# Differences of decay sums on POOL and more convolution taps on VectorE, in a two-layer GLA, convolution and MoE trunk

## The chip, the cores and the metric

The kernel runs on one core of one Trainium2 chip. The metric is the device time of one execution in microseconds (us), given as the median of several runs. The engines are named as in the profile: PE is TensorE (matmul), PEld its weight loads, DVE is VectorE, ACT is ScalarE, POOL is GpSimd, SP is SyncE.

## What is computed

Two layers over 256 tokens of width 1024, all in float32. Each layer runs a token mixer and then a channel mixer (a dense SwiGLU in layer 0, a top-2-of-8 mixture of experts in layer 1). The change lies in the token mixer, which is, cut to what matters:

```
z = h @ w_in                        # q, k, v, g, gate rank, ca, cb
log_a = log_sigmoid(gr @ w_gate_up + b_gate) / 16
bc = cumsum(log_a)                  # "decay sums", along the tokens
decay[i, j] = exp(bc_i - bc_j)      # for j <= i
attn = einsum(q, k, decay);  o = attn @ v (+ carried state);  o = rmsnorm(o) * silu(g)

u = ca * sigmoid(cb)                # 512 channels
u = causal_dwconv(u, conv_w) + b    # 31 taps, each channel by itself
u = silu(layernorm(u))
x = x + concat([o, u]) @ w_out
```

## The kernel before

**Weights.** Every weight is loaded by SP in units of 1 MB. ACT copies a unit to `w_hi` (L463), DVE writes the remainder to `w_lo` (L755, `lo(n)`, a `tensor_tensor` whose two inputs both lie in SBUF), and PE multiplies with both. The mixer has ten input units (`in_unit`, `tokens`) and four output units (`down_unit`).

**Attention by levels.** The masked attention of a layer is put together from nine levels, `LEVELS = [128, 64, 32, 16, 8, 4, 2, 1, 0]`. For level n the decay sums `cum` (128 x 512) are cut in blocks of 2s, and every element is subtracted from, or has subtracted from it, the block's reference element. `differences(n)` does this with two instructions of 128 x 256 (L832, L833; one instruction, L825, for n = 0), so 15 instructions in a layer. ACT takes the exponential in place (`decays(n)`, L503), DVE multiplies q by it (`q_decayed(n)`, L841, 128 x 512), POOL multiplies k by it (L423, 128 x 512), PE forms the products (`level(n)`, L1336). The first three results go out through ACT, the levels 3 to 8 through DVE (`level_read_out(n)`, L852: two `copy_predicated`, data from PSUM, mask from SBUF). After level 8 is read out, PE multiplies the attention by v (L1380 to L1382).

**Convolution.** The 512 channels are four tiles. A tap on DVE is one `scalar_tensor_tensor` of 128 x 256 (L810: `acc = cu * tap + acc`, `cu` and `acc` in SBUF; the first tap of a tile is L806). A tap on PE is a matmul of a diagonal matrix, which ACT makes (L544), with the input (L1312, two records a tap). DVE has all 31 taps of the tiles 0 and 1 and the first 19 of tile 2; PE has 12 of tile 2 and all 31 of tile 3, so 43. Every DVE tap waits for the tap before it on the same tile (`conv_step[c]`).

**What sets the order.** Each engine's program is written out by hand. In DVE's program of a mixer, `lo`, `q_decayed`, `differences`, `conv_input` (L796), `level_read_out` and batches of taps `conv(count)` alternate; PE's program has `conv(3)` behind levels 2 to 7, `conv(4)` behind level 8, `conv(16)` behind the products with v, and the remainder behind the transposes (L1390). POOL's program of a mixer is the eight multiplications of k, and two loads of norm weights. `Difs` and `qkE` have two buffers each, used by even and odd n, so that `differences(n)` waits until q and k of level n - 2 are multiplied.

**Around the end of the mixer.** When the products with v are done: ACT squares them (L605), DVE sums (L922), ACT takes the root (L609), DVE scales and gates (L932), PE transposes (L1390), ACT and DVE write `t_hi` and `t_lo` (L612, L937), and PE starts the output projection (`down_unit`, L1259). In the middle of the first output unit PE sums the convolution's channels (L1401) and for that all taps must be done.

Of the kernel before, what the change touches and what calls it, by code (L numbers as in the profile page):

```python
# [21 lines left out]
ALU = mybir.AluOpType  # L22
# [3 lines left out]
P = 128  # L26
# [8 lines left out]
def trunk(nc, x, ln1_w, w_in, w_gate_up, b_gate, gla_norm_w, conv_w, conv_b, cn_w, cn_b, w_out,  # L35
          ln2_w, wd_gate, wd_up, wd_down, w_router, we_gate, we_up, we_down, final_norm_w, out):
    _, T, D = x.shape
# [3 lines left out]
    TAPS, CH = conv_w.shape[1:]  # L41
# [51 lines left out]
    with ctx:  # L93
# [3 lines left out]
        def on(stack):  # L97
# [171 lines left out]

        BY_VECTOR = 19
        LATE = TAPS - BY_VECTOR
        DVE_CONV = ([(c, w) for w in range(LATE) for c in (0, 1)]
                    + [(c, w if c < 2 else w - LATE) for w in range(LATE, TAPS) for c in (0, 1, 2)])
        PE_CONV = [(3, w) for w in range(TAPS)] + [(2, w) for w in range(BY_VECTOR, TAPS)]
        STEPS = [TAPS, TAPS, BY_VECTOR + 1, 1]
        IN_BANK = [0, 1, 2, 0, 1, 2, 0, 1, 2, 0]
# [100 lines left out]
        def _(pool):  # L379
# [32 lines left out]
            for l in range(L):  # L412

                if l:
                    pool.wait_ge(added, 2 * TT)
                pool.memset(cu[:, :, 0:PAD], 0.0).then_inc(pads_ready, 1)
                pool.memset(att[:], 0.0).then_inc(pads_ready, 1)

                for n in range(len(LEVELS) - 1):
                    pool.wait_ge(decay_ready, 8 * l + n + 1)  # L420
                    if n >= 2:
                        pool.wait_ge(level_done, 9 * l + n - 1)
                    pool.tensor_tensor(qkE[n % 2][:, 1], qk[:, 1], Difs[:, n % 2], ALU.mult).then_inc(kE_ready, 1)  # L423
                pool.wait_ge(level_done, 9 * (l + 1))
                pool.dma_start(lnw[:], norm_weights[2 * l + 1].partition_broadcast(P)).then_inc(lnw_ready, 16)
                pool.wait_ge(normed, TT * (2 * l + 2))
                pool.dma_start(lnw[:], norm_weights[2 * l + 2].partition_broadcast(P)).then_inc(lnw_ready, 16)
# [319 lines left out]
        def _(dve):  # L747
            def lo(n, item=None):

                slot, _ = slot_use(n)  # L750
                if item is None:
                    dve.wait_ge(hi_ready, n + 1)
                else:
                    dve.wait_ge(hi_ready, item * N_FF + (n + 1))
                dve.tensor_tensor(w_lo[slot][:], raw[slot][:], w_hi[:, hi_slot(n), :].bitcast(F32), ALU.subtract).then_inc(lo_ready, 1)  # L755
# [34 lines left out]
            def mixer(l):  # L790
                b = BASE[l]

                def conv_input(g):
                    dve.wait_ge(cgate_ready, 2 * l + g + 1)
                    dve.wait_ge(pads_ready, 2 * (l + 1))
                    dve.tensor_tensor(cu[:, 2 * g:2 * g + 2, PAD:], cgate, WB[IN_BANK[U_C + 2 * g]][:].rearrange("p (c t) -> p c t", c=2),  # L796
                                      ALU.mult).then_inc(cu_ready, 1)
# [3 lines left out]
                def conv(count):  # L801

                    for c, w in DVE_CONV[done[0]:done[0] + count]:
                        if w == 0:
                            dve.wait_ge(cu_ready, 2 * l + c // 2 + 1)
                            dve.tensor_scalar(acc[:, c, :], cu[:, c, 0:T], taps[:, l, 0, c:c + 1],  # L806
                                              pv[:, l, PV_CB + c:PV_CB + c + 1], ALU.mult, ALU.add).then_inc(conv_step[c], 1)
                        else:
                            dve.wait_ge(conv_step[c], STEPS[c] * l + w)
                            dve.scalar_tensor_tensor(out=acc[:, c, :], in0=cu[:, c, w:w + T], scalar=taps[:, l, w, c:c + 1],  # L810
                                                     in1=acc[:, c, :], op0=ALU.mult, op1=ALU.add).then_inc(conv_step[c], 1)
                    done[0] += count


                def differences(n):

                    s = LEVELS[n]
                    Dif = Difs[:, n % 2]
                    if n == 0:
                        dve.wait_ge(cum_ready, l + 1)  # L820
                    if n >= 2:
                        dve.wait_ge(kE_ready, 8 * l + n - 1)
                        dve.wait_ge(qE_ready, 8 * l + n - 1)
                    if s == P:
                        dve.tensor_tensor(Dif[:, :, 0:P], cum[:, :, P - 1:P].broadcast_to([P, KT, P]), cum[:, :, 0:P],  # L825
                                          ALU.subtract).then_inc(dif_ready, 1)
                        return
                    nb = KT * T // (2 * s)
                    blocks = cum[:].rearrange("p k (b s) -> p (k b) s", s=2 * s)
                    dst = Dif.rearrange("p k (b s) -> p (k b) s", s=2 * s)  # L830
                    ref = blocks[:, :, s - 1:s].broadcast_to([P, nb, s])
                    dve.tensor_tensor(dst[:, :, 0:s], ref, blocks[:, :, 0:s], ALU.subtract)  # L832
                    dve.tensor_tensor(dst[:, :, s:], blocks[:, :, s:], ref, ALU.subtract).then_inc(dif_ready, 1)  # L833

                def q_decayed(n):
                    dve.wait_ge(decay_ready, 8 * l + n + 1)
                    if n == 0:
# [37 lines left out]
                        c = cum[:, k, P * t:P * (t + 1)]  # L875
                        ins = dve.tensor_tensor_scan(c, ones[:], c, 0.0, ALU.mult, ALU.add)
                ins.then_inc(cum_ready, 1)
                differences(0)
                differences(1)
                lo(b + 7)  # L880
                q_decayed(0)
                lo(b + 8)
                q_decayed(1)
                conv_input(0)
                conv(6)
                differences(2)
                lo(b + 9)
                conv(4)
                q_decayed(2)
                differences(3)  # L890
                lo(b + 10)
                conv(4)
                conv_input(1)
                q_decayed(3)
                differences(4)
                conv(6)
                lo(b + 11)
                q_decayed(4)
                differences(5)
                conv(8)  # L900
                lo(b + 12)
                level_read_out(3)
                q_decayed(5)
                differences(6)
                conv(7)
                lo(b + 13)
                level_read_out(4)
                q_decayed(6)
                differences(7)
                conv(10)  # L910
                level_read_out(5)
                q_decayed(7)
# [287 lines left out]
        def _(pe):  # L1200
# [79 lines left out]
            def mixer(l):  # L1280
# [25 lines left out]
                def conv(count):  # L1306

                    for c, w in PE_CONV[done[0]:done[0] + count]:
                        m = len(PE_CONV) * l + done[0]
                        bank = WB[3][:, 0:T] if c == 3 else WB[3][:, T:2 * T]  # L1310
                        pe.wait_ge(diag_ready, m + 1)
                        pe.matmul(bank, diag[:, done[0] % DIAGS, :], cu[:, c, w:w + T], start=(w in (0, BY_VECTOR) and (c == 3) == (w == 0)),  # L1312
                                  stop=(w == TAPS - 1)).then_inc(diag_used, 1)
                        done[0] += 1
# [66 lines left out]
                    pe.matmul(WB[1][:, vs], attx[:, r, hp, :], v[:, 0, vs], start=True, stop=False)  # L1381
                    ins = pe.matmul(WB[1][:, vs], att[:, r, 2 + hp, :], v[:, 1, vs], start=False, stop=True)  # L1382
                ins.then_inc(o_done, 1)
                conv(16)
                pe.wait_ge(o_gated, l + 1)
                for hd in range(HEADS):
                    for t in range(TT):
# [182 lines left out]
```

## Time and profile before

| | |
|---|---|
| median of 3 runs | 1306.63 us (1305.07 to 1307.05) |
| the profiled execution, its own time | 1306.7 us |
| its span from first to last instruction | 1304.9 us |
| busy share of the span | PE 96%, PEld 82%, DVE 79%, ACT 64%, POOL 6% |
| mean granted clock of TensorE | 0.983 of full |
| mixer of layer 0, by the timeline | roughly 16 to 145 us |
| mixer of layer 1, by the timeline | roughly 354 to 480 us |

The engine's busy share is over the whole span: the mixers take about a fifth of it, the dense channel mixer and the experts the rest. In a timeline row the first number is the start and the second the duration, both in us; an engine's neighbouring instructions of one kind are merged into a row (x6), and then the second number reaches from the first one's start to the last one's end. DVE instructions of this kernel overlap their neighbours by some 0.08 us.

### The profile page before, as it was taken

The page shows a single profiled execution, that of the slowest core. Times are in us where ns is not written, and L with a number is a line of the kernel's source. Part 1 is how long each engine was busy: PE and PEld are TensorE (multiplying, and loading weights), DVE is VectorE, ACT ScalarE, POOL GpSimd, SP SyncE. Part 2 cuts the span into 40 slices and gives each one's busy share as a digit, 9 for nine tenths or more (in the row PEclk, how much of TensorE's full clock was granted, in tenths as well). Part 3 has the DMA queues.
Part 4 walks back from the last instruction along what each step waited for, and adds up shares of the span by engine and source line. Part 5 has one row for each costly group of instructions (what it writes and reads, how often), then busy time and mean ns, then how long its engine had stood idle before and what let it go on. Part 6 is the DMA issues. An engine that isn't in the chain of part 4 may idle for free.

```text
span 1304.9 us, 18713 instructions
## 1 busy us (share of the span) xinstructions
PE 1251.0 (96%) x6911; PEld 1067.8 (82%) x6911; DVE 1036.2 (79%) x963; ACT 832.4 (64%) x755; POOL 84.4 (6%) x75
## 2 busy tenths in 40 slices
PE   5998899999799987999999999999999999999997
PEld 5997799999699876888888888888888888888885
DVE  5898654444569967989989989989989989989986
ACT  5754643333476545677677677677677677677674
POOL 3250000000013100000000000000000000000000
PEclk9999899999899998999999999999999999999998
DMA  9940455555434234999999999999999999999970
GB/s 275 331 130 17 145 187 174 189 194 176 147 102 158 82 129 146 337 386 355 335 388 353 336 387 354 338 385 354 337 386 353 338 385 354 340 384 352 338 292 32
DMA packets 180166, 351.69 MB, mean 270 GB/s; under 512 B 8678, under 2 KB 68380, under 8 KB 180124
## 3 DMA queue, kind: packets, MB, share of 16 engines
q1 hardware_dynamic: 178108, 343.77, 75.3%
q0 software_dynamic: 2016, 7.34, 1.5%
q8 instruction: 29, 0.48, 0.2%
q14 instruction: 13, 0.11, 0.0%
HBM read 348.99 MB, written 2.10 MB: 269 GB/s over the span
## 4 chain that ended last, share of the span: by engine, by line
PE 90%; DVE 7%; ACT 2%; issue 1%; DMA 0%; SPq 0%; DVEq 0%; ACTq 0%
PE YB L1517 19%; PE WBS L1504 12%; PE WBS L1505 12%; PE WBS L1506 12%; PE YB L1259 8%; PE WBS L1222 5%; PE WBS L1223 5%; PE WBS L1224 5%; DVE w_lo L755 2%; PE WBS L1312 2%; DVE acc L810 2%; PE YB L1532 1%; PE WBS L1271 1%; PE YB L1336 1%; PE WBS L1234 1%
## 5 line engine op out<-in xcount | busy, mean ns | idle before, releaser
L755 DVE TENSOR_TENSOR w_lo<-raw,w_hi 128x2048 fp32r<-128x2048 f32 x325 | 741.1, 2296 | 113.1 <-ACT w_hi L463 109.6
L463 ACT ACTIVATE w_hi<-raw 128x2048 fp32r<-128x2048 f32 x325 | 616.4, 1915 | 143.8 <-PE WBS L1506 67.2
L1504 PE MATMUL WBS<-w_hi,t_hi 128*128 128x512 f32 (+1 forms) x768 | 290.6, 378 | 2.0 <-DVE t_lo L1152 2.0
L1505 PE MATMUL WBS<-w_lo,t_hi 128*128 128x512 f32 (+1 forms) x768 | 285.8, 372 | 0.0
L1506 PE MATMUL WBS<-w_hi,t_lo 128*128 128x512 f32 (+1 forms) x768 | 285.7, 372 | 0.0
L1504 PEld LDWEIGHTS WBS<-w_hi,t_hi 128*128 128x128 f32 x768 | 144.5, 188 | 26.8 <-issue 2.1
L1506 PEld LDWEIGHTS WBS<-w_hi,t_lo 128*128 128x128 f32 x768 | 144.4, 188 | 26.3
L1505 PEld LDWEIGHTS WBS<-w_lo,t_hi 128*128 128x128 f32 x768 | 144.6, 188 | 24.4
L1222 PE MATMUL WBS<-t_hi,w_lo 128*128 128x256 f32 x544 | 157.3, 289 | 6.5 <-DVE w_lo L755 4.9
L1223 PE MATMUL WBS<-t_hi,w_hi 128*128 128x256 f32 x544 | 156.2, 287 | 0.0
L1224 PE MATMUL WBS<-t_lo,w_hi 128*128 128x256 f32 x544 | 156.0, 287 | 0.0
L1517 PE MATMUL YB<-w_hi,eT_hi 128*128 128x512 f32 x352 | 114.6, 407 | 1.0
L1222 PEld LDWEIGHTS WBS<-t_hi,w_lo 128*128 128x128 f32 x544 | 106.8, 196 | 9.1 <-issue 7.9
L1517 PE MATMUL YB<-w_lo,eT_hi 128*128 128x512 f32 x352 | 111.0, 396 | 0.0
L1517 PE MATMUL YB<-w_hi,eT_lo 128*128 128x512 f32 x352 | 110.8, 396 | 0.0
L1223 PEld LDWEIGHTS WBS<-t_hi,w_hi 128*128 128x128 f32 x544 | 106.9, 197 | 0.4
L1224 PEld LDWEIGHTS WBS<-t_lo,w_hi 128*128 128x128 f32 x544 | 106.8, 196 | 0.0
L1517 PEld LDWEIGHTS YB<-w_hi,eT_hi 128*128 128x128 f32 x352 | 62.0, 188 | 25.0 <-issue 13.9
L1517 PEld LDWEIGHTS YB<-w_hi,eT_lo 128*128 128x128 f32 x352 | 66.4, 189 | 16.2
L1517 PEld LDWEIGHTS YB<-w_lo,eT_hi 128*128 128x128 f32 x352 | 66.2, 188 | 16.2
L665 ACT ACTIVATE dT_hi<-dact 128x512 fp32r<-128x512 f32 x11 | 7.0, 632 | 111.2 <-PE YB L1259 106.3
L810 DVE SCALAR_TENSOR_TENSOR acc<-cu,taps,acc 128x256 f32<-128x256 f32 x156 | 71.4, 524 | 0.0
(243 smaller groups left out, 1324.1 us busy)
## 6 DMA issues: line engine op xcount, KB each, us to landing
raw<-in_we_gate SPq DMA_DIRECT2D x88, 1024.0 KB, 5.3
raw<-in_we_up SPq DMA_DIRECT2D x88, 1024.0 KB, 5.3
raw<-in_we_down SPq DMA_DIRECT2D x88, 1024.0 KB, 5.2
raw<-in_w_in SPq DMA_DIRECT2D x20, 1024.0 KB, 5.5
raw<-in_wd_gate SPq DMA_DIRECT2D x11, 1024.0 KB, 5.4
raw<-in_wd_up SPq DMA_DIRECT2D x11, 1024.0 KB, 5.3
raw<-in_wd_down SPq DMA_DIRECT2D x11, 1024.0 KB, 4.8
raw<-in_w_out SPq DMA_DIRECT2D x8, 1024.0 KB, 11.0
```

What stands on the lines that cost most here:

```text
L463: act.activation(w_hi[:, hi_slot(n), :], raw[slot][:], ACT.Copy).then_inc(hi_ready, 1)
L755: dve.tensor_tensor(w_lo[slot][:], raw[slot][:], w_hi[:, hi_slot(n), :].bitcast(F32), ALU.subtract).then_inc(lo_ready, 1)
L810: dve.scalar_tensor_tensor(out=acc[:, c, :], in0=cu[:, c, w:w + T], scalar=taps[:, l, w, c:c + 1], in1=acc[:, c, :], op0=ALU.mult, op1=ALU ...
L1222: pe.matmul(dst, lo[:, k, cols], a_hi[:, k, :], start=(k == 0), stop=False)
L1223: pe.matmul(dst, hi[:, k, cols], a_hi[:, k, :], start=False, stop=False)
L1224: ins = pe.matmul(dst, hi[:, k, cols], a_lo[:, k, :], start=False, stop=(k == KD - 1))
L1259: ins = pe.matmul(YB[:, 2 * t + half, :], a[:, k0 + k, tok], w[:, k, HALF * half:HALF * (half + 1)], start=(first and k == 0 and s), stop= ...
L1312: pe.matmul(bank, diag[:, done[0] % DIAGS, :], cu[:, c, w:w + T], start=(w in (0, BY_VECTOR) and (c == 3) == (w == 0)), stop=(w == TAPS - ...
L1504: pe.matmul(bank, xs_hi[:, k0 + k, :], hi[:, k, :], start=start, stop=False)
L1505: pe.matmul(bank, xs_hi[:, k0 + k, :], lo[:, k, :], start=False, stop=False)
L1506: ins = pe.matmul(bank, xs_lo[:, k0 + k, :], hi[:, k, :], start=False, stop=stop)
L1517: ins = pe.matmul(YB[:, half, :], a[:, f, :], w[:, k, HALF * half:HALF * (half + 1)], start=(first and s), stop=(last and e))
```

## The change

POOL issues the differences for all levels: 0 and 1 at the start of its mixer program, and `differences(n + 2)` right behind its multiplication of k at level n. They are the same instructions on the same data, with the same waits. DVE loses them. Tile 2 of the convolution has 27 taps on DVE in place of 19, so DVE has 89 taps in a layer (81 before) and PE 35 (43 before). The batches of taps in DVE's program grow: 67 taps stand ahead of the read-out of level 8, where there were 55, and 22 behind it, where there were 26. The last 8 taps are all on tile 2. PE's batch behind the products with v is 12 (16 before), and the last batch has 1 (5 before). ACT makes 35 diagonals (43 before).

```
-        BY_VECTOR = 19
-        LATE = TAPS - BY_VECTOR
-        DVE_CONV = ([(c, w) for w in range(LATE) for c in (0, 1)]
-                    + [(c, w if c < 2 else w - LATE) for w in range(LATE, TAPS) for c in (0, 1, 2)])
+        BY_VECTOR = 27
+        LATE = 12
+        DVE_CONV = [(c, w) for w in range(LATE) for c in (0, 1)]
+        for w in range(BY_VECTOR):
+            DVE_CONV += [(c, w + LATE) for c in (0, 1) if w + LATE < TAPS] + [(2, w)]
...
 (POOL's program)
+                def differences(n):
+                    s = LEVELS[n]
+                    Dif = Difs[:, n % 2]
+                    if n >= 2:
+                        pool.wait_ge(kE_ready, 8 * l + n - 1)
+                        pool.wait_ge(qE_ready, 8 * l + n - 1)
+                    if s == P:
+                        pool.tensor_tensor(Dif[:, :, 0:P], cum[:, :, P - 1:P].broadcast_to([P, KT, P]), cum[:, :, 0:P],
+                                           ALU.subtract).then_inc(dif_ready, 1)
+                        return
+                    nb = KT * T // (2 * s)
+                    blocks = cum[:].rearrange("p k (b s) -> p (k b) s", s=2 * s)
+                    dst = Dif.rearrange("p k (b s) -> p (k b) s", s=2 * s)
+                    ref = blocks[:, :, s - 1:s].broadcast_to([P, nb, s])
+                    pool.tensor_tensor(dst[:, :, 0:s], ref, blocks[:, :, 0:s], ALU.subtract)
+                    pool.tensor_tensor(dst[:, :, s:], blocks[:, :, s:], ref, ALU.subtract).then_inc(dif_ready, 1)
+
+                pool.wait_ge(cum_ready, l + 1)
+                differences(0)
+                differences(1)
                 for n in range(len(LEVELS) - 1):
                     pool.wait_ge(decay_ready, 8 * l + n + 1)
                     if n >= 2:
                         pool.wait_ge(level_done, 9 * l + n - 1)
                     pool.tensor_tensor(qkE[n % 2][:, 1], qk[:, 1], Difs[:, n % 2], ALU.mult).then_inc(kE_ready, 1)
+                    if n + 2 < len(LEVELS) - 1:
+                        differences(n + 2)
...
 (DVE's program: its own differences() is gone, and of the order)
-                differences(0)
-                differences(1)
                 lo(b + 7)
                 q_decayed(0)
                 lo(b + 8)
                 q_decayed(1)
                 conv_input(0)
+                conv(8)
+                lo(b + 9)
                 conv(6)
-                differences(2)
-                lo(b + 9)
-                conv(4)
                 q_decayed(2)
-                differences(3)
                 lo(b + 10)
-                conv(4)
+                conv(6)
                 conv_input(1)
                 q_decayed(3)
-                differences(4)
-                conv(6)
+                conv(8)
                 lo(b + 11)
                 q_decayed(4)
-                differences(5)
-                conv(8)
+                conv(10)
                 lo(b + 12)
                 level_read_out(3)
                 q_decayed(5)
-                differences(6)
-                conv(7)
+                conv(9)
                 lo(b + 13)
                 level_read_out(4)
                 q_decayed(6)
-                differences(7)
                 conv(10)
...
 (PE's program, behind the products with v)
-                conv(16)
+                conv(12)
```

## Rows read from the trace of the kernel before

**Rows 1.** The page: the chain that ended last, by engine.
```profile
PE 90%; DVE 7%; ACT 2%; issue 1%; DMA 0%; SPq 0%; DVEq 0%; ACTq 0%
```

**Rows 2.** Windows: length, busy us of PE, PEld, DVE, ACT, POOL, clock, DMA.
```profile
75.00:90.00 15.00, 15.00 (x129) 14.17 (x128) 15.00 (x25) 5.50 (x11) 7.01 (x3) 1.00 0.43 141
...
105.00:110.00 5.00, 3.08 (x18) 2.78 (x17) 5.00 (x12) 0.74 (x2) 0.00 (x0) 0.80 0.31 108
```

**Rows 3.** Timeline of DVE, and one row of ACT, layer 0.
```profile
46.04 2.29 DVE L755 TENSOR_TENSOR w_lo<-raw,w_hi 128x2048 fp32r<-128x2048 f32 x1 [0.58 <-ACT w_hi L463]
...
49.96 3.38 DVE L755 TENSOR_TENSOR w_lo<-raw,w_hi 128x2048 fp32r<-128x2048 f32 x1
...
55.23 1.67 DVE L810 SCALAR_TENSOR_TENSOR acc<-cu,taps,acc 128x256 f32<-128x256 f32 x4
...
59.69 2.71 DVE L810 SCALAR_TENSOR_TENSOR acc<-cu,taps,acc 128x256 f32<-128x256 f32 x4
...
93.14 0.42 DVE L833 TENSOR_TENSOR Difs<-cum 128x256 f32<-128x256 f32 x1
93.48 4.04 DVE L810 SCALAR_TENSOR_TENSOR acc<-cu,taps,acc 128x256 f32<-128x256 f32 x10
93.60 0.63 ACT L503 ACTIVATE Difs<-Difs 128x512 f32<-128x512 f32 x1 [5.78 <-DVE Difs L833]
97.43 1.35 DVE L852 COPY_PREDICATED att<-masks,YB 128x512 f32<-128x512 uint8 x2
```

**Rows 4.** Timeline of POOL: multiplications of k, layers 0 and 1.
```profile
49.45 1.74 POOL L423 TENSOR_TENSOR lnw<-qk,Difs 128x512 f32<-128x512 f32 x1
58.31 2.61 POOL L423 TENSOR_TENSOR qkE<-qk,Difs 128x512 f32<-128x512 f32 x1 [7.12 <-ACT Difs L503]
...
71.26 6.09 POOL L423 TENSOR_TENSOR qkE<-qk,Difs 128x512 f32<-128x512 f32 x1 [4.24 <-ACT Difs L503]
...
94.37 4.29 POOL L423 TENSOR_TENSOR lnw<-qk,Difs 128x512 f32<-128x512 f32 x1 [2.18 <-ACT Difs L503]
...
434.84 1.28 POOL L423 TENSOR_TENSOR lnw<-qk,Difs 128x512 f32<-128x512 f32 x1 [6.42 <-PE YB L1336]
```

**Rows 5.** Timeline of POOL, mask building: s = 64, then s = 1.
```profile
3.24 0.25 POOL L400 TENSOR_SCALAR_AFFINE_SELECT mask_f<-mask_f 128x64 f32<-128x64 f32 x1
...
9.50 0.16 POOL L399 MEMSET mask_f<- 128x64 f32 x1
...
11.52 0.65 POOL L402 TENSOR_SCALAR_AFFINE_SELECT mask_f<-mask_f 128x64 f32<-128x64 f32 x1
```

**Rows 6.** Timeline of DVE and PE, layer 1, last levels.
```profile
434.73 1.36 DVE L852 COPY_PREDICATED att<-masks,YB 128x512 f32<-128x512 uint8 x2 [0.99 <-PE YB L1336]
...
444.58 0.46 PE L1380 MATMUL WBS<-v,att 128*128 128x128 f32 x2 [0.21 <-DVE att L852]
```

**Rows 7.** Timeline of PE: products with v, layer 0 and layer 1.
```profile
108.80 0.63 PE L1382 MATMUL WBS<-v,att 128*128 128x128 f32 x2
109.23 0.63 PE L1380 MATMUL WBS<-v,att 128*128 128x128 f32 x2
...
445.99 0.39 PE L1380 MATMUL WBS<-v,att 128*128 128x128 f32 x2
446.21 0.39 PE L1381 MATMUL WBS<-v,attx 128*128 128x128 f32 x2
```

**Rows 8.** Timeline of DVE and PE behind the products, layer 0.
```profile
118.07 2.46 DVE L810 SCALAR_TENSOR_TENSOR acc<-cu,taps,acc 128x256 f32<-128x256 f32 x6
119.14 1.04 PE L1390 MATMUL WBS<-ident,qk 128*128 128x128 f32 x8
...
121.36 1.28 DVE L937 SCALAR_TENSOR_TENSOR t_lo<-WBS,pv,t_hi 128x1024 fp32r<-128x1024 f32 x1 [0.83 <-ACT t_hi L612]
...
122.56 2.46 DVE L810 SCALAR_TENSOR_TENSOR acc<-cu,taps,acc 128x256 f32<-128x256 f32 x6
...
125.12 0.42 DVE L944 TENSOR_TENSOR acc<-acc,WBS 128x256 f32<-128x256 f32 x1
```

More of the change, by code:

```diff
@@ L812, in conv @@
                     done[0] += count
[L815 to L833, printed above, removed]
                 def q_decayed(n):
```

## The prediction

> **What bounds the kernel now.** I read the page first, for the chain that ended last: PE holds 90% of it and DVE 7% [rows 1]. PE's part is the experts and the dense mixer, which the change doesn't touch. So the question is where DVE's 7%, some 90 us, lies. The chain in order of time puts it in the two mixers: in layer 0 it runs on DVE from 48 us to 107 us without a break. The windows say the same: from 75 to 90 us DVE is busy 15.00 of 15.00 us, and from 105 to 110 us DVE is busy throughout, while PE is down to 3.08 of 5.00 us [rows 2]. In layer 0 the read-out of level 8 is therefore as late as DVE's work ahead of it is long, and PE's products with v wait for it. In layer 1 the two engines run neck and neck: DVE has one pause of 0.99 us, waiting for PE, and PE waits only 0.21 us for the last read-out [rows 6].
>
> Behind the mixers no one catches up what they lose: PE is the chain there. So what the mixers gain or lose is the kernel's.
>
> The third view was POOL's timeline, since POOL gets the work. A multiplication of 128x512 takes 1.28 us when DVE leaves it alone, but 1.74, 2.61, 4.29 and 6.09 us elsewhere [rows 4]. DVE shows the counterpart: four taps take 1.67 us, but 2.71 us where POOL's instruction of 58.31 us ends (at 60.92 us), and `lo` takes 2.29 us, but 3.38 us while POOL's second multiplication runs [rows 3, 4]. That is 1.04 and 1.09 us of standstill, nearly all of POOL's 1.28 us. So one POOL multiplication costs DVE about what it takes, and the two engines take turns. Only the read-outs (data from PSUM, one input in SBUF) run beside it at their usual pace: POOL's instruction of 94.37 us ends 1.23 us after the read-out of 97.43 us began, and that pair takes its usual 1.35 us [rows 3, 4].
>
> The Trainium skill states such a rule (SBUF — State Buffer, Who interferes with whom): a DVE instruction with two SBUF inputs and a GpSimd instruction that reads SBUF exclude each other for a whole instruction, the later one blocking. The trace agrees in the standstill of 1.04 and 1.09 us. It differs in the other direction: by that rule POOL would get its turn when the current DVE instruction ends, and its 6.09 us span several.
>
> **The change part by part, for one layer, up to the read-out of level 8.**
>
> Differences off DVE. One starts at 93.14 us and what follows it at 93.48 us, so one costs 0.34 us [rows 3]. The 12 of levels 2 to 7 stand in the gapless part: 12 x 0.34 = 4.1 us less. The first three stood ahead of a wait: `lo` at 46.04 us had waited 0.58 us for ACT's `w_hi` [rows 3], which starts no sooner, so they give nothing.
>
> Taps on DVE. Ten taps take 4.04 us with one lone tap at some 0.47, so each further one 0.396 us [rows 3]. Twelve more stand ahead of the read-out (67 for 55): 4.75 us more. DVE's own work ahead of the read-out is thus longer by 0.7 us. This alone shows that the differences were traded for taps one for one, and anything POOL takes comes on top.
>
> Differences on POOL. The trace has no POOL instruction of this form. From the nearest row, the multiplication with 512 elements and a standstill of 1.04 to 1.09 us, one of 256 elements blocks DVE for 0.52 us if all of it goes by the element, and for 1.07 us if nothing does. Alone a multiplication takes 1.28 us and blocks for most of it, so most goes by the element; I take 0.55 us. Twelve of them: 6.6 us. Some find cover in read-outs and in the two `conv_input` (PSUM data). A read-out pair is 1.35 us [rows 3], but the k multiplications already use some of these; I take off two diffs' and a bit's worth, 1.3 us: 5.3 us. The bounds are 12 x 0.52 with half of it covered, 3.1 us, and 12 x 1.07, 12.8 us. Of the first three, the last may still run when `lo` wants to start: 0.3 us (between 0 and 0.55).
>
> Short rows. At s = 1 the differences walk 256 rows of one element. POOL's memset at s = 1 takes 0.16 us, no sign of a cost; its affine select goes from 0.25 us at s = 64 to 0.65 us at s = 1, so 0.40 us for 63 more rows, 6.3 ns each [rows 5]. Over the levels 2 to 7 there are 2 x (8 + 16 + 32 + 64 + 128 + 256) = 1008 rows, so between 0 and 6.4 us. The select works out an index for each element, which a subtraction doesn't; I take a value near the memset's end, 0.5 us.
>
> Behind the products with v. PE's transposes start at 119.14 us, once its batch of 16 taps is through, though DVE's gating is over when the taps at 118.07 us start [rows 8]. With 12 taps they start up to 1.1 us sooner. But DVE's six taps there are now all on tile 2, each waiting for the last. The one such handover in view, from the last tap (122.56 + 2.46 = 125.02) to the addition at 125.12 [rows 8], has a gap of 0.10 us where neighbours otherwise overlap by 0.08. So each link costs about 0.12 to 0.18 us, five links 0.6 to 0.9 us. DVE's `t_lo`, which had waited 0.83 us for ACT [rows 8], is now late by DVE's own taps. What is left of the 1.1 us is 0.3 us. The remaining taps (2 for 6), PE's four fewer and ACT's eight fewer diagonals lie beside the output projection and give nothing: PE's first half unit covers them, and the channel sums follow it.
>
> Layer 0: 0.7 + 5.3 + 0.3 + 0.5 - 0.3 = +6.5 us.
>
> Layer 1 has the same terms, with two differences. DVE's pause of 0.99 us takes up 1.0 us of them. Against that, PE is no longer kept busy. In layer 0, where PE waited for DVE, the products with v ran at the lower granted clock (0.80 of full as the mean of 105 to 110 us [rows 2]), 0.43 us from group to group, and 0.22 us in layer 1 [rows 7]. If layer 1 comes to wait like layer 0, its groups run at the slower pace too: nearly nine of the twelve at 0.21 us more, 1.8 us. Layer 1: 6.5 - 1.0 + 1.8 = +7.3 us.
>
> The sum is made on the profiled execution's 1306.7 us (span 1304.9), within 0.1 us of the median: 1306.7 + 6.5 + 7.3 = 1320.5 us.
>
> The Trainium skill has a figure for POOL's rate (GPSIMD Engine Reference, section 3.1: 4497 ns for 2048 elements). With the row of 1.28 us for 512 that makes 2.1 ns an element, so 0.75 us for one difference as an estimate, of which some 0.6 us would block; the sum would be 1321 or 1322 us by it.
>
> **The rivals.**
>
> *POOL's chain becomes late (1334 us).* Each level now needs three turns of POOL in a row (k, and two differences two levels on), and POOL's waits for a turn reached 6.09 us [rows 4]. DVE needs some 7 to 8 us a level. If a turn is refused through a whole batch of taps, `q_decayed` stands still until the second difference (0.55), ACT's exponential (0.63) and a part of the k multiplication (1.28) are done [rows 3, 4]. That is some 2 us a level, of which 0.55 is counted already, so 1.3 to 1.4 us more on five levels, 6.7 us a layer: 1320.5 + 13.4 = 1334 us. For it: the batches of taps, where POOL was refused, grow from 6 to 8 and from 8 to 10. Against: while DVE stands still POOL gets its turn at once, so that it heals itself. Short rows at the select's price would end at about the same time (2 x 5.9 more, 1332 us). Together 0.27.
>
> *All of it is covered (1306 us).* If the differences fall in read-outs, `conv_input` and waits, +5.3 and the layer-1 clock go, and 2 x (0.7 + 0.5 - 0.3) - 1.0 is left, with 0.3 us twice: 1308 us; with links of taps at no cost 1306 us. It decides once 9 or more of 12 find cover. Against: the read-outs start only at level 3, and k multiplications fill them. 0.06.
>
> *Faster (1302 us).* The other side: POOL's new order pushes the k multiplications of levels 2 to 5, which stand DVE still now, into read-outs. Each is worth 1.04 us, three a layer would give 6 us against 1308. It needs all differences covered as well. 0.04.
>
> **How the numbers follow.** Forecast 0.63, late POOL or short rows 0.27, covered 0.06, faster 0.04. The forecast's own range: with 3.1 us in place of 5.3, no short rows and no loss of clock 1306.7 + 3.8 + 2.8 = 1313; with 0.75 us a difference and 2 us of short rows about 1328. The range that leaves out 2 in 10 goes from 1311 to 1337 us. Within 0.2% is 2.6 us, about what a measurement can tell. Faster 0.04, same 0.06, slower 0.90.
>
> **What would show it.** Right: after DVE's `cum`, POOL shows 15 instructions of 128x256 a layer, of 0.7 us where alone and up to some us elsewhere; DVE is still without a gap up to level 8, its batches of taps and its `lo` have standstills of about 0.55 us at more places than before, and the read-out of level 8 is 6 to 7 us later after `cum` than now; in layer 1 the products with v pace at 0.43 us. The late-POOL rival would show as DVE's idle time ahead of L841, released by ACT's L503. Wrong: taps beside POOL's differences at their usual 0.396 us. Then broadcast or short subtractions don't exclude DVE, and the time is near 1308 us.

## The result, and the profile after

The changed kernel takes 1320.6 us (median of 4 runs, 1318.16 to 1321.47) where the kernel before takes 1306.01 us (4 runs): a ratio of 1.0113, 95% interval 1.01 to 1.0126, 14.6 us slower. The forecast was 1320.5 us. The profiled execution took 1318.16 us, its span is 1316.4 us, 11.5 us longer than that of before.

The page's chain that ended last, by engine:

```profile
PE 81%; DVE 12%; ACT 3%; issue 2%; SPq 2%; DMA 1%; DVEq 0%; ACTq 0%
```

DVE's share has risen from 7% to 12% [rows 1]. The windows of the changed kernel, which answer to [rows 2]:

```profile
75.00:90.00 15.00, 15.00 (x133) 14.33 (x132) 15.00 (x23) 4.31 (x7) 3.20 (x5) 1.00 0.21 72
...
105.00:110.00 5.00, 4.15 (x24) 3.36 (x25) 5.00 (x12) 0.81 (x3) 0.00 (x0) 0.66 0.00 0
```

DVE is busy in both from end to end. From 105 to 110 us it is still on its way to the read-out of level 8, and PE's granted clock is already down. DVE's timeline in layer 0, from the decay sums (L880) to that read-out, the counterpart of [rows 3] (L779 is `lo`, L845 the multiplication of q, L830 a tile's first tap, L834 a tap, L856 a read-out):

```profile
42.64 1.37 DVE L880 TENSOR_TENSOR_SCAN cum<-ones,cum 128x128 f32<-128x128 f32 x4
45.71 2.30 DVE L779 TENSOR_TENSOR w_lo<-raw,w_hi 128x2048 fp32r<-128x2048 f32 x1 [1.70 <-ACT w_hi L487]
47.94 1.78 DVE L845 TENSOR_TENSOR qkE<-qk,Difs 128x512 f32<-128x512 f32 x1
...
51.85 1.10 DVE L845 TENSOR_TENSOR lnw<-qk,Difs 128x512 f32<-128x512 f32 x1
...
53.58 1.94 DVE L830 TENSOR_SCALAR acc<-cu,taps,pv 128x256 f32<-128x256 f32 x2
55.44 3.90 DVE L834 SCALAR_TENSOR_TENSOR acc<-cu,taps,acc 128x256 f32<-128x256 f32 x6
...
61.46 2.45 DVE L834 SCALAR_TENSOR_TENSOR acc<-cu,taps,acc 128x256 f32<-128x256 f32 x6
...
66.64 4.25 DVE L834 SCALAR_TENSOR_TENSOR acc<-cu,taps,acc 128x256 f32<-128x256 f32 x6
...
72.01 4.31 DVE L834 SCALAR_TENSOR_TENSOR acc<-cu,taps,acc 128x256 f32<-128x256 f32 x6
...
79.76 5.87 DVE L834 SCALAR_TENSOR_TENSOR acc<-cu,taps,acc 128x256 f32<-128x256 f32 x10
...
89.58 5.40 DVE L834 SCALAR_TENSOR_TENSOR acc<-cu,taps,acc 128x256 f32<-128x256 f32 x9
...
98.93 5.05 DVE L834 SCALAR_TENSOR_TENSOR acc<-cu,taps,acc 128x256 f32<-128x256 f32 x10
...
112.11 1.33 DVE L856 COPY_PREDICATED att<-masks,YB 128x512 f32<-128x512 uint8 x2
```

Six undisturbed taps take 2.45 us (61.46), the batches beside it 3.90, 4.25 and 4.31 us. Ten take 5.87 and 5.05 us where ten took 4.04 us. The read-out ends at 113.44 us, 69.43 us after the decay sums, where it was 62.66 us after them (44.33 to 106.99 us). What POOL does meanwhile, the counterpart of [rows 4] (L435 and L436 are the differences, L445 the multiplication of k):

```profile
44.67 0.61 POOL L435 TENSOR_TENSOR Difs<-cum 128x256 f32<-128x256 f32 x1
45.24 0.62 POOL L436 TENSOR_TENSOR Difs<-cum 128x256 f32<-128x256 f32 x1
...
79.99 0.73 POOL L435 TENSOR_TENSOR Difs<-cum 128x256 f32<-128x256 f32 x1 [4.74 <-DVE qkE L845]
80.68 0.79 POOL L436 TENSOR_TENSOR Difs<-cum 128x256 f32<-128x256 f32 x1
81.69 1.28 POOL L445 TENSOR_TENSOR lnw<-qk,Difs 128x512 f32<-128x512 f32 x1 [0.22 <-ACT Difs L527]
...
89.80 0.73 POOL L435 TENSOR_TENSOR Difs<-cum 128x256 f32<-128x256 f32 x1 [6.83 <-DVE lnw L845]
90.49 0.79 POOL L436 TENSOR_TENSOR Difs<-cum 128x256 f32<-128x256 f32 x1
91.24 1.48 POOL L445 TENSOR_TENSOR qkE<-qk,Difs 128x512 f32<-128x512 f32 x1
98.35 1.79 POOL L445 TENSOR_TENSOR lnw<-qk,Difs 128x512 f32<-128x512 f32 x1 [5.63 <-PE YB L1332]
```

Three turns of POOL lie inside the ten taps of 79.76 us, which take 1.83 us more than ten undisturbed ones. POOL starts the next differences when DVE has multiplied q, so at most levels just as DVE begins its taps, and the k multiplication follows into the same taps.

In layer 1 the counterpart of [rows 6], the decay sums and the read-out of level 5, shows DVE without a pause:

```profile
384.53 1.37 DVE L880 TENSOR_TENSOR_SCAN cum<-ones,cum 128x128 f32<-128x128 f32 x4
...
444.92 1.31 DVE L856 COPY_PREDICATED att<-masks,YB 128x512 f32<-128x512 uint8 x2
...
453.11 1.33 DVE L856 COPY_PREDICATED att<-masks,YB 128x512 f32<-128x512 uint8 x2
```

The last read-out ends at 454.44 us, 68.54 us after the decay sums, where it was 62.78 us after them.

### The profile page after: what moved, and what is told of

It reads as the page before. It is cut to its first block, busy times and chain, and to the rows that moved or that the text cites. A ratio compares the mean times of both kernels' runs of the same rounds, so it can differ in the third digit from the quotient of the medians.

```text
span 1316.4 us, 18649 instructions
## 1 busy us (share of the span) xinstructions
PE 1249.3 (95%) x6879; PEld 1064.6 (81%) x6879; DVE 1045.1 (79%) x949; ACT 826.9 (63%) x739; POOL 95.3 (7%) x105
## 4 chain that ended last, share of the span: by engine, by line
PE 81%; DVE 12%; ACT 3%; issue 2%; SPq 2%; DMA 1%; DVEq 0%; ACTq 0%
PE YB L1513 19%; PE WBS L1500 12%; PE WBS L1501 12%; PE WBS L1502 12%; PE YB L1255 8%; DVE acc L834 5%; PE WBS L1218 4%; PE WBS L1219 3%; PE WBS L1220 3%; DVE w_lo L779 3%; PE YB L1528 1%; DVE att L856 1%; DMA raw<-in_w_in 1%; SPq L321 1%; PE WBS L1267 1%
## 5 line engine op out<-in xcount | busy, mean ns | idle before, releaser
L779 DVE TENSOR_TENSOR w_lo<-raw,w_hi 128x2048 fp32r<-128x2048 f32 x325 | 738.9, 2289 | 115.1 <-ACT w_hi L487 111.4
L834 DVE SCALAR_TENSOR_TENSOR acc<-cu,taps,acc 128x256 f32<-128x256 f32 x172 | 89.9, 582 | 0.4
```

## The experiments

Two lengths tell most, both read off the profiled executions: from the end of the decay sums to the end of the last read-out in layer 0 (A0) and in layer 1 (A1). The ratio compares a kernel with the kernel before as measured in the same set of runs.

| kernel | A0 | A1 | median us | ratio to before, 95% interval |
|---|---|---|---|---|
| before | 62.66 | 62.78 | 1305.0 to 1306.0 in four sets | |
| changed | 69.43 | 68.54 | 1320.6 | 1.0113 (1.01, 1.0126) |
| changed, once more | 69.33 | 68.54 | 1319.58 | 1.0113 (1.0096, 1.0129) |
| POOL's part alone | 65.12 | 62.79 | 1306.99 | 1.0017 (1.0007, 1.0026) |
| the taps alone | 67.34 | 67.37 | 1318.07 | 1.0102 (1.0085, 1.0119) |
| POOL only writes | 62.38 | 62.78 | 1305.6 | 1.0003 (0.9991, 1.0016) |
| POOL copies | 66.54 | 65.61 | 1313.46 | 1.0068 (1.0051, 1.0085) |
| k on DVE | 59.54 | 62.78 | 1302.64 | 0.9978 (0.9969, 0.9988) |

### The two halves of the change, each alone

```
e1: POOL's program as changed; BY_VECTOR = 19, conv(16), DVE's batches as before
e2: DVE keeps its differences(n); BY_VECTOR = 27, conv(12), DVE's batches as changed
```

> The differences on POOL as in the changed kernel, the taps split 81 to 43 and batched as in the kernel before. Theory (POOL and DVE take turns): DVE loses 12 x 0.34 us of its own per layer and gets about 6.2 us of new standstills (read off the changed kernel's DVE timeline), so the read-out of level 8 is about 2.2 us later after the decay sums in layer 0 and 1.2 us in layer 1, behind it nothing changes: 1306.0 + 3.4 = 1309.5 us, give or take 2 for the granted clock. Rival (the taps alone are the cost, POOL's work is free): DVE is 4 us shorter in layer 0 and PE-bound in layer 1, 1301 us.

> The taps split 89 to 35 and batched as in the changed kernel, the differences on DVE as before. Theory: DVE has 12 x 0.396 = 4.75 us more ahead of the read-out of level 8, no new standstills; behind it about 0.6 us less a layer, and 1 us of layer 1 goes into DVE's pause: 1306.0 + 4.1 + 3.1 = 1313 us. Rival (POOL's part is the whole cost, PE's relief pays for the taps): within 1 us of 1306.

POOL's part alone gives A0 +2.46 us, as the theory says, and A1 nothing, where 1.2 us was expected. In layer 1 DVE still pauses ahead of level 5's read-out, as long as before (1.05 us for 0.99):

```profile
434.19 1.35 DVE L855 COPY_PREDICATED att<-masks,YB 128x512 f32<-128x512 uint8 x2 [1.05 <-PE YB L1331]
```

So the pause has taken up nothing. DVE's standstills in that layer, added up, grow from 5.3 to 9.3 us, which is no more than the 4.1 us of its own that DVE loses, because POOL's last three multiplications of k still end beside read-outs. In all +1.5 us, 1306.99 us where 1309.5 was expected.

The taps alone give A0 +4.68 us and A1 +4.59 us. A1 was expected at +3.75 us: the pause is used up there, but POOL's multiplication of k at level 5, which cost DVE nothing before, now meets taps and costs 1.03 us.

In time the halves add up: 1.5 + 12.6 = 14.1 us for the 14.1 to 14.6 of the whole. In the mixers they do so only roughly, 7.1 us for 6.8 in A0 and 4.6 us for 5.8 in A1: with the taps in place POOL's part costs layer 1 another 1.2 us. Both rivals fall: POOL's work isn't free, and the taps aren't paid for by PE. The theory was right on A0 and too low on the time of the second (1313 for 1318.07 us). Less than 1 us of the missing 5 is in A1; the others come up again below.

### What makes DVE stand still

```
e3: pool.memset(dst[:, :, 0:s], 0.0); pool.memset(dst[:, :, s:], 0.0)             # n >= 2
e4: pool.tensor_copy(dst[:, :, 0:s], blocks[:, :, 0:s]); the same for [:, :, s:]  # n >= 2
```

> The changed kernel with POOL's differences of the levels 2 to 7 replaced by memsets of the same 128x256 pieces: POOL writes as much, at the same places and behind the same waits, but reads nothing; the decay of those levels is left out of the result. Theory (what excludes DVE is the shared read side): the standstills of 0.36 to 0.47 us vanish, those of 1.04 us under the k multiplications stay; 4.2 + 3.3 us less than the changed kernel's 1320.6, so 1313 us. Rival (any POOL instruction on SBUF excludes DVE, or POOL's chain of waits is the cost): 1319 us or more, with standstills of about 0.3 us.

> The changed kernel with POOL's differences of the levels 2 to 7 replaced by copies of the same pieces of the decay sums (one input read in place of two); the subtraction of the reference element is left out. Theory: a read excludes DVE for as long as it lasts, so standstills stay at the same places and are shorter, about 0.25 us each: 1316 to 1318 us. Rival (only instructions of POOL with two inputs exclude DVE): 1313 us, as without any read.

With memsets, POOL's and DVE's timelines (L436 and L437 are the memsets, L449 the k multiplication):

```profile
77.76 0.34 POOL L436 MEMSET Difs<- 128x256 f32 x1 [5.12 <-DVE qkE L849]
78.03 0.34 POOL L437 MEMSET Difs<- 128x256 f32 x1
78.71 6.25 POOL L449 TENSOR_TENSOR lnw<-qk,Difs 128x512 f32<-128x512 f32 x1 [0.34 <-ACT Difs L531]
```

```profile
77.56 4.04 DVE L838 SCALAR_TENSOR_TENSOR acc<-cu,taps,acc 128x256 f32<-128x256 f32 x10
81.52 2.28 DVE L783 TENSOR_TENSOR w_lo<-raw,w_hi 128x2048 fp32r<-128x2048 f32 x1
83.73 1.36 DVE L860 COPY_PREDICATED att<-masks,YB 128x512 f32<-128x512 uint8 x2
```

Two memsets run inside ten taps that take their undisturbed 4.04 us. So POOL's writes don't hold DVE up. These memsets are short; a longer one in the kernel before says the same. It is still running when a DVE instruction with two inputs in SBUF starts, and that one takes the 1.28 us that its like takes at 356.04 us, where POOL does nothing:

```profile
354.23 0.95 POOL L417 MEMSET att<- 128x1024 f32 x1
354.65 1.28 DVE L766 SCALAR_TENSOR_TENSOR h<-X,rstd,lnw 128x1024 f32<-128x1024 f32 x1
```

The k multiplication behind the two memsets is refused for 5 us, through taps and `lo`, and gets its turn beside the read-out. With copies, which read one input, POOL and DVE show:

```profile
78.18 0.54 POOL L436 COPY Difs<-cum 128x256 f32<-128x256 f32 x1 [4.73 <-DVE qkE L849]
78.65 0.64 POOL L437 COPY Difs<-cum 128x256 f32<-128x256 f32 x1
80.35 1.52 POOL L449 TENSOR_TENSOR lnw<-qk,Difs 128x512 f32<-128x512 f32 x1 [1.06 <-ACT Difs L531]
```

```profile
77.97 5.38 DVE L838 SCALAR_TENSOR_TENSOR acc<-cu,taps,acc 128x256 f32<-128x256 f32 x10
```

Ten taps stand still for 1.34 us: 1.03 for the k multiplication, so 0.31 for the two copies, 0.15 each, where a subtraction costs 0.36 us. So it is POOL's reading that DVE stands still for, longer with two inputs. A0 falls by 2.9 us against the changed kernel. Added up over layer 0, DVE stands still 1.7 us for copies where it stood still 4.2 us for subtractions, which is 2.5 us of it. The time, 1313.46 us, is the one that the rival gave (1313 us, a single read costs nothing), but 0.15 us at every copy is not nothing: here the rows decide, and the theory's 0.25 us for a copy was too much.

The memsets save more than was expected: 1305.6 us in place of 1313, A0 62.38. The expectation had kept all k multiplications at 1.04 us. But without the differences' turns, those of the levels 5 to 7 cost DVE nothing; in the kernel before, the one of 94.37 us ended beside a read-out too [rows 3, 4]. Against the changed kernel A0 falls by 7.1 us: 4.2 us are the subtractions' own standstills, and 2.9 us are three k multiplications. So a good third of it was indirect: the differences set the pace of POOL's queue and pulled the k multiplications into taps.

The Trainium skill states this side of the rule too (SBUF — State Buffer, Who interferes with whom): a GpSimd instruction that only writes doesn't contend with a DVE instruction with two SBUF inputs. The traces agree (0.00 us with memsets, 0.15 and 0.36 us with one and two reads).

### The chain of the last eight taps

```
e8: FIRST = [(c, w) for w in range(TAPS) for c in (0, 1)]; HEAD = len(FIRST) - BY_VECTOR
    DVE_CONV = FIRST[:HEAD] + [tap for w in range(BY_VECTOR) for tap in (FIRST[HEAD + w], (2, w))]
```

> The changed kernel with DVE's 89 taps in another order: 35 of the tiles 0 and 1 first, then tile 2 always in turn with them, so that the last 8 are no chain on one tile. Nothing else differs. Theory (each link of the chain costs 0.12 to 0.18 us on the way to t_lo): the output projection starts 0.6 us sooner after the sums of squares in each layer, 1 to 1.5 us in all: 1319.3 us. Rival (the links cost nothing that counts): no change in that stretch.

DVE behind the products, changed kernel, then without the chain (L933 and L932 are `t_lo`):

```profile
122.89 3.08 DVE L834 SCALAR_TENSOR_TENSOR acc<-cu,taps,acc 128x256 f32<-128x256 f32 x6
125.89 1.28 DVE L933 SCALAR_TENSOR_TENSOR t_lo<-WBS,pv,t_hi 128x1024 fp32r<-128x1024 f32 x1
```

```profile
124.48 2.45 DVE L833 SCALAR_TENSOR_TENSOR acc<-cu,taps,acc 128x256 f32<-128x256 f32 x6
126.89 1.28 DVE L932 SCALAR_TENSOR_TENSOR t_lo<-WBS,pv,t_hi 128x1024 fp32r<-128x1024 f32 x1
```

Five links cost 0.63 us, 0.126 us each. From the sums of squares to the output projection it is 9.56 us in the changed kernel, 8.99 us here: 0.57 us a layer, as expected. Yet the time is 1320.12 us, which can't be told from the changed kernel's. This trace has the products with v of layer 0 and the output projection of both layers in part at the lower clock, which the changed kernel's first trace has not. Windows over the same stretches of the kernel without the chain:

```profile
113.40:119.30 5.90, 5.65 (x30) 5.55 (x31) 3.93 (x11) 1.05 (x2) 0.00 (x0) 0.71 0.02 5
128.30:142.00 13.70, 13.70 (x54) 11.36 (x55) 6.92 (x8) 3.74 (x5) 0.00 (x0) 0.88 0.24 77
```

and over those of the changed kernel:

```profile
113.40:117.70 4.30, 4.00 (x30) 3.90 (x31) 3.97 (x11) 1.05 (x3) 0.00 (x0) 1.00 0.23 86
...
127.30:141.00 13.70, 13.70 (x61) 11.44 (x62) 7.64 (x8) 4.61 (x8) 0.00 (x0) 1.00 0.22 77
```

From the read-out to the sums of squares it is 5.90 us at a clock of 0.71 and 4.27 us at full clock. From the start of layer 0's output projection to the end of the residual additions it is 28.80 and 27.27 us, in layer 1 28.84 and 27.25 us. Each such stretch costs about 1.6 us.

### Is it PE's idle time that brings the lower clock?

```
e5:  12 x pe.matmul(WB[1][:, 0:P], ones[:], ones[:])   ahead of level 7
e10: the same, and 10 x pe.matmul(WB[2][:, 0:P], ones[:], ones[:])   ahead of the output projection
```

> The changed kernel with 12 matmuls of ones by ones (128x128 each, into a PSUM bank that is free then) on PE ahead of level 7, where its trace shows PE idle for 3.58 us in layer 0 and waiting in layer 1 too. Their results are overwritten, nothing else is changed. Theory (the changed kernel loses more than its mixers' 9.4 us because PE's longer waits leave TensorE a lower granted clock in parts that nobody changed): the mean clock rises from 0.977 to 0.98 towards 0.983 and the time falls by 2 to 5 us, to 1316 to 1318. Rival (the parts nobody changed differ for another reason, or by the state of the chip): 1320 to 1321 us, clock 0.977 to 0.98.

> The changed kernel once more, unaltered, for a second trace beside the runs of this set. Theory (some stretches behind PE's long waits run at the lower granted clock, each at about 1.6 us, and where such a stretch falls differs from run to run): 1318 to 1321.5 us, and this trace shows other stretches slow than the first one did, with the read-outs of level 8 again at 69.4 and 68.5 us after the decay sums. Rival (all that the kernel loses is fixed in its work): the same stretches at the same clock.

> The changed kernel with PE kept busy in two waits: 12 matmuls of ones ahead of level 7, as in the run with one such batch, and 10 more ahead of the output projection, where PE is idle for 2.7 us in the changed kernel. Results are overwritten. Theory (idle PE in the second wait is what lets the output projection run at the lower clock): the output projection takes 27.25 us in both layers, and the runs stay near the lowest of the changed kernel, 1317 to 1319 us. Rival (these waits have no part in it): 1320 us, as the changed kernel.

With PE busy ahead of level 7 the time is 1319.72 us (1.0116, interval 1.0096 to 1.0136); with both waits filled it is 1319.78 us (1.0107, 1.009 to 1.0124). The mean clock of a run rises from 0.977 - 0.98 to 0.98 - 0.982, but the time does not fall by anything that four runs can show. With both waits filled the output projection does take the expected 27.26 us in both layers, but in that trace the products with v of layer 0 have part of the lower clock (5.60 us from read-out to sums of squares, for 4.27). So these waits don't bring the loss as a whole; a gain of 1 us would not be seen here. The changed kernel's second trace has A0 and A1 as the first (69.33, 68.54), and this time the output projection of layer 0 in part at the lower clock, 28.85 us for 27.27. So which stretches get the lower clock differs between executions of one kernel. The dummy matmuls lengthened nothing either.

### A faster version, and two that weren't

If a k multiplication on POOL costs DVE 1.04 us or more, it is cheaper on DVE, together with q:

```
e6: # DVE, levels 0 to 5; POOL keeps k at the levels 6 and 7
    dve.tensor_tensor(qkE[n % 2], qk[:], Difs[:, n % 2].unsqueeze(1).broadcast_to([P, 2, KT, T]), ALU.mult)
e7: e6, with BY_VECTOR = 25, tile 2 in turn with the others; DVE's batches ahead of level 5's read-out
    grown by 4 taps, DVE's last one ahead of t_lo by 2, PE's behind the levels 6 to 8 2, 2, 2
    (3, 3, 4 before), conv(14) behind the products
e9: e6, with BY_VECTOR = 21 and conv(14) in place of conv(16)
```

> The kernel before, with q and k of the levels 0 to 5 multiplied by one DVE instruction of 1024 elements, and POOL multiplying k at the levels 6 and 7 alone, where it ran beside read-outs. Theory (a k multiplication on POOL holds DVE up for 1.04 to 1.12 us; on DVE it adds 0.53 us): in layer 0 six standstills go, 6.3 us, and 3.2 us of DVE work come, so the read-out of level 8 is about 3 us sooner after the decay sums unless PE is then the bound, which its 2.2 us of idle time there says; in layer 1 PE's work already sets 62.78 us and nothing is gained. In all 2 to 3 us faster than the kernel before. Rival (POOL's work was free after all): DVE gets 3.2 us longer a layer, 3 to 5 us slower.

> As the run before it, and 6 taps of tile 2 moved from PE to DVE (87 to 37), 18 of PE's taps ahead of the products with v in place of 22, 14 right behind them in place of 16, 59 of DVE's ahead of the last read-out in place of 55, and tile 2 always in turn with another tile so that no tap waits for the one just before it. Theory: PE's part ahead of the read-out is 4 x 0.43 = 1.7 us shorter, which lets layer 1 gain as well; layer 0 is DVE-bound at 62.7 - 3.1 + 1.6 = 61.2 us, layer 1 near 61.1 us; behind the products about 0.9 us less a layer: 1305.5 - 4.8 = 1300.7 us, and less if the clock gains. Rival (the kernel before was balanced, taps on DVE cost as much as they give): 1305 us or more.

> The kernel with k multiplied by DVE at the levels 0 to 5, and two taps of tile 2 moved from PE's batch behind the products with v (14 for 16) to the end of DVE's (83 to 41). Theory (there DVE's t_lo and PE's transposes have a wait to fill): the output projection starts up to 0.9 us sooner, DVE's last taps hold the channel sums back by some 0.4 us of it, so 0.5 us a layer: 1 us faster than with k on DVE alone, 1301.6 us. Rival (DVE's last taps cost as much as PE's sooner start gives): no difference that can be measured.

> The kernel with k multiplied by DVE at the levels 0 to 5 once more, on the chip of this set. Theory: again 2 to 3 us faster than the kernel before (ratio 0.998). Rival (the first set's 2.4 us was the clock's luck): within 1 us.

With k on DVE the kernel takes 1302.64 us, and in the other set 1302.0 us (0.9972, interval 0.9962 to 0.9981). It beats the kernel before by 2.4 and 3.4 us in the two sets, and the changed kernel by 18 us. DVE in layer 0 and in layer 1:

```profile
48.11 1.22 DVE L840 TENSOR_TENSOR qkE<-qk,Difs 128x1024 f32<-128x1024 f32 x1
49.25 2.28 DVE L754 TENSOR_TENSOR w_lo<-raw,w_hi 128x2048 fp32r<-128x2048 f32 x1
...
430.06 1.35 DVE L854 COPY_PREDICATED att<-masks,YB 128x512 f32<-128x512 uint8 x2 [1.76 <-PE YB L1339]
```

`lo` behind the first multiplication takes 2.28 us where it took 3.38 [rows 3]. A0 falls by 3.12 us, as expected. A1 stays at 62.78 us, as expected too: DVE waits there 1.76 us for level 5.

Moving taps on top brought nothing: 1305.57 us (1.0005, 0.9994 to 1.0017) where 1300.7 was expected. In layer 0 POOL's last two k multiplications, which had run beside read-outs, now met taps:

```profile
86.59 1.38 DVE L805 TENSOR_SCALAR acc<-cu,taps,pv 128x256 f32<-128x256 f32 x1
...
92.61 5.05 DVE L809 SCALAR_TENSOR_TENSOR acc<-cu,taps,acc 128x256 f32<-128x256 f32 x10
```

1.38 us for 0.40 and 5.05 us for 4.04: 2.0 us of standstill that I had priced at nothing, and A0 is 63.10 us for the 61.2 expected. In layer 1 A1 is 62.77 us though PE has 4 taps less. DVE waits for level 5, and then four read-outs with ten taps between them run without a gap, while PE waits 1.92 us for the last. The end of layer 1's levels is bound by level 5 on PE and then by DVE, and the taps would have to move from behind level 5's read-out to ahead of it; that wasn't tried. The two taps at the other end (1300.84 us; 0.9973, 0.996 to 0.9985) can't be told from k on DVE alone (1302.0 us in the same set). The output projection starts 0.87 us sooner, but PE then waits for DVE's longer last batch, and from there to the residual's end it takes 0.79 us longer, where 0.4 was expected:

```profile
116.95 3.25 DVE L809 SCALAR_TENSOR_TENSOR acc<-cu,taps,acc 128x256 f32<-128x256 f32 x8
```

```profile
120.98 1.97 PE L1404 MATMUL WBS<-acc,ones 128*128 128x256 f32 x8 [0.86 <-DVE acc L946]
```

## Why the prediction was right, point by point

**The path.** Right. DVE's work ahead of the last read-out decides layer 0, with DVE unbroken from `lo` on. In layer 1 the changed kernel has used up the pause of 0.99 us, as forecast: DVE stands still 11.5 us there for 5.3 before, and 6.2 us more of it, 0.7 of own work and 1.0 less of pause make 5.9 us for the measured 5.76.

**Ahead of the last read-out.** Forecast +6.8 us in layer 0 (0.7 + 5.3 + 0.3 + 0.5) and +5.8 in layer 1; measured +6.77 and +5.76 us. The own work is as priced: the taps alone lengthen layer 0 by 4.68 us for 4.75. POOL's price is right as a sum, not in its parts. Adding up the disturbed rows of layer 0 against undisturbed ones, DVE stands still 12.4 us, against 6.3 us before: 6.1 us more for the 5.3 + 0.3 + 0.5 forecast. But a subtraction costs 0.36 to 0.47 us, not 0.55, and 11 of 12 did so where two and a bit were forecast to be covered: 4.2 us in place of 5.3. The 0.3 us for the first three did not come: `lo` takes 2.30 us behind them. The other 1.9 us are the k multiplications of the levels 6 and 7, which lost the cover of the read-outs (8 of them cost DVE time, for 6 before). That mechanism isn't in the prediction, so that the sum comes out is luck. The allowance for short rows was not needed: the pair with rows of one element (89.80 us) takes 0.73 and 0.79 us, exactly as the pair with rows of two (79.99 us).

**Behind the products.** The 0.3 us left by the chain of taps is right: 9.86 us before, 9.56 after, and the links measured 0.126 us each. That the last 2 taps (6 before) give nothing was wrong by 0.28 us a layer: from the output projection's start to the residual's end it is 27.27 us for 27.55, since the channel sums had waited for the last tap.

**The clock.** This term failed in its place. Forecast was +1.8 us for layer 1's products at the lower clock, because PE would wait there. Its groups ran at full clock in all traces of the changed kernel, and in the first trace so did layer 0's, which had the lower one before [rows 7]: the read-out to sums of squares fell from 5.89 to 4.27 us. Work alone is 6.77 + 5.76 - 0.3 x 2 - 0.28 x 2 = +11.4 us. The first pair of traces differs by 11.5 us, the medians by 14.6. That 11.4 and 11.5 agree is chance too: between these two traces the products of layer 0 gave 1.6 us back, and parts outside of the mixers took 2.1 us. The taps alone show the same surplus: 8.1 us of work by A0, A1 and the two terms behind, 12.6 us of time. The 3 us between would fit the lower-clock stretches of 1.6 us, which fall now here, now there, and parts that nobody changed; the runs beside the profiled ones left only their mean clock, 0.977 to 0.98 in the changed kernel and 0.983 to 0.986 before, so this is argued and not shown. Counted from layer 0's decay sums on, without the two stretches from decay sums to residual, the profiled executions have 1050.2 us before, 1052.3 and 1052.1 us in the changed kernel's two, and 1050.6 and 1048.4 us in the two of the kernel with k on DVE, so that executions of one kernel differ here by as much as the two kernels do. A window of 20 us behind the second mixer, where the router starts, is one example of a lower clock; before, then changed:

```profile
486.00:506.00 20.00, 13.88 (x81) 12.31 (x82) 13.56 (x62) 6.68 (x12) 2.50 (x7) 0.74 0.36 130
```

```profile
495.50:515.50 20.00, 13.70 (x68) 10.95 (x68) 13.12 (x61) 5.42 (x10) 2.51 (x7) 0.66 0.37 131
```

What makes these stretches more frequent in the kernels with the longer mixers stays open: filling two of PE's waits didn't bring the time back.

**The number.** 1320.5 us for 1320.6 is closer than the account behind it. Forecast were 12.0 us of work and 1.8 us of clock in layer 1's products; the runs have 11.4 us of work, nothing in that place, and some 3 us elsewhere. The work ahead of the last read-out was forecast well; the last microseconds agree by luck.

**The rivals.** Late POOL: no. DVE never waits at `q_decayed` for a difference; the wait of up to 6 us that I had taken for a risk doesn't occur, since POOL's differences came just as DVE began its taps and got their turn at the next tap, or came as DVE began `lo` and had it behind that (2.53 us). Covered: the memset run shows what that would have given, 1305.6 us, with one k multiplication fewer in DVE's way than before. Faster by cover for k: the opposite came.

## What to carry to other kernels

Work moved from DVE to POOL isn't off DVE: in these traces DVE stood still for an instruction of POOL that reads SBUF when its own instruction had two inputs in SBUF, and not for one that only writes. Here a subtraction cost DVE 0.34 us on DVE itself and 0.36 to 0.47 us on POOL, and a multiplication of 512 elements 0.54 us against 1.04. Before such a move, compare the row of the moved operation with a row of DVE stretched by POOL, and look what else in POOL's queue now lands elsewhere. Even a trade of one unit of work for another on the engine that bounds must be counted ahead of the point that others wait for, and not over the whole kernel: 8 more taps were 12 more ahead of the last read-out, and they alone lengthened the way to it by 4.7 us in one layer and 4.6 us in the other. The time grew by more, 12.6 us, and that remainder is not explained.

## What was not expected of the hardware

- A tap's first form (`tensor_scalar`, one SBUF tensor input and per-partition scalars) stands still for POOL as well: two take 1.94 us where two took 0.74 us in the kernel with k on DVE, and one 1.38 us for 0.40.
- POOL's turn comes at the next DVE instruction (0.73 us for a subtraction, 0.61 alone, and 2.53 us where that meant the end of `lo`) or only after 2 to 5 us and several instructions: a k multiplication, 1.28 us alone, took 3.31 us (417.64 us, POOL's part alone), 4.29 and 6.09 us [rows 4] and 6.25 us (78.71 us, memsets). The subtractions that came just behind DVE's multiplication of q got their turn at the next instruction. What decides inside a batch of taps stays open.
- Rows of one element cost a POOL subtraction nothing, though its affine select grew with them [rows 5].
- In the mixers the lower granted clock came in stretches that cost about 1.6 us each (5.90 us for 4.27, 28.80 us for 27.27), at other places in another execution of the same kernel.
